# The first mixer's matrix products as three rounded products, with half of the modulation in later mixers

## What is computed

```python
proj = x @ w_in
da_q, da_k, da_v, r_q, r_k, r_v, r_g, m_q, gate_logits = split(proj)
y_da = diff_attention(da_q, da_k, da_v, ...)          # 8 heads, two softmaxes each
y_ret = silu(r_g) * retention(r_q, r_k, r_v, ...)     # 4 heads, a norm each
m_k, m_v = split(mem @ w_mem_kv)
y_mem = memory_attention(m_q, m_k, m_v)               # 4 heads
gates = sigmoid(gate_logits + b_gate)
merged = sum(gates[n] * (y[n] @ w_branch[n]) for n in range(3))
x = layer_norm(alpha * x + merged @ w_o)
```

## Time and profile before

| | |
|---|---|
| median of 3 runs | 2375.59 us (2375.39 to 2376.65) |
| the profiled execution | 2377.7 us, its span 2375.9 us |
| PE busy | 2269.4 us, 96% of the span |
| DVE busy | 1608.5 us, 68% |
| ACT busy | 1297.5 us, 55% |
| DMA | 638.14 MB, mean 269 GB/s |

### The profile page before, as it was taken

How to read it: one execution, slowest core, us unless ns; L and a number is a source line. 1 busy time by engine, 2 the same in 40 slices (tenths; PEclk the granted TensorE clock), 3 DMA queues, 4 the chain that set the end, 5 groups by cost and what they waited for, 6 DMA issues and landing times.

```text
span 2375.9 us, 25462 instructions
## 1 busy us (share of the span) xinstructions
PE 2269.4 (96%) x10290; PEld 1857.8 (78%) x10290; DVE 1608.5 (68%) x1897; ACT 1297.5 (55%) x1562; POOL 0.4 (0%) x6
## 2 busy tenths in 40 slices
PE   8999999998999979799989899999999999999997
PEld 7668877887888866578848788888888888888886
DVE  0266233546889863345423698989898998989895
ACT  1245113105677743334320587877777787878784
POOL 0000000000000000000000000000000000000000
PEclk9999999997999999999999799999999999999999
DMA  8465455745998862045440498999999898989892
GB/s 345 185 255 213 178 212 233 274 195 223 359 356 327 325 266 107 1 177 213 161 176 1 194 391 335 365 347 354 349 353 377 325 372 327 374 328 376 326 374 96
DMA packets 51217, 638.14 MB, mean 269 GB/s; under 512 B 8737, under 2 KB 10638, under 8 KB 12302
## 3 DMA queue, kind: packets, MB, share of 16 engines
q1 hardware_dynamic: 48526, 630.33, 69.1%
q10 hardware_dynamic: 2560, 6.03, 0.7%
HBM read 635.29 MB, written 1.05 MB: 268 GB/s over the span
## 4 chain that ended last, share of the span: by engine, by line
PE 91%; DVE 4%; ACT 2%; DMA 2%; issue 1%; SPq 0%; DVEq 0%; ACTq 0%
PE psum L1697 56%; PE psum L1487 19%; PE psum L1479 5%; PE psum L1707 2%; PE psum L1581 2%; PE psum L1720 2%; PE psum L1787 2%; DMA ring<-w_in 1%; DMA ring<-w_branch_in 1%; DVE stage_lo L1338 1%; PE psum L1592 0%; ACT arena L546 0%; DMA ring<-w_in_in 0%; DVE arena L559 0%; PE psum L1509 0%
## 5 line engine op out<-in xcount | busy, mean ns | idle before, releaser
L1338 DVE TENSOR_TENSOR stage_lo<-ring,stage_hi 128x1024 fp32r<-128x1024 f32 (+1 forms) x934 | 1109.6, 1218 | 107.4 <-ACT stage_hi L926 82.7
L926 ACT ACTIVATE stage_hi<-ring 128x1024 fp32r<-128x1024 f32 (+1 forms) x934 | 965.3, 1056 | 279.0 <-PE psum L1697 247.9
L1697 PE MATMUL psum<-stage_hi,x_hi 128*128 128x512 f32 (+1 forms) x1344 | 529.1, 394 | 14.2 <-DVE x_lo L1320 11.5
L1697 PE MATMUL psum<-stage_hi,x_lo 128*128 128x512 f32 (+1 forms) x1344 | 522.3, 389 | 0.0
L1697 PE MATMUL psum<-stage_lo,x_hi 128*128 128x512 f32 (+1 forms) x1344 | 521.1, 388 | 0.0
L1697 PEld LDWEIGHTS psum<-stage_hi,x_hi 128*128 128x128 f32 x1344 | 253.2, 188 | 64.1 <-issue 11.9
L1697 PEld LDWEIGHTS psum<-stage_hi,x_lo 128*128 128x128 f32 x1344 | 253.0, 188 | 53.0
L1697 PEld LDWEIGHTS psum<-stage_lo,x_hi 128*128 128x128 f32 x1344 | 253.5, 189 | 49.3
L1697 PE MATMUL psum<-stage_hi,h_hi 128*128 128x512 f32 x664 | 259.9, 391 | 4.8 <-DVE h_lo L1377 4.8
L1697 PE MATMUL psum<-stage_lo,h_hi 128*128 128x512 f32 x664 | 258.6, 389 | 0.0
L1487 PE MATMUL psum<-arena,ring 128*128 128x256 f32 x1024 | 227.0, 382 | 6.3 <-DVE arena L1285 4.3
(11 more groups left out here) (210 smaller groups left out, 1764.5 us busy)
## 6 DMA issues: line engine op xcount, KB each, us to landing
ring<-moe_w_gate_in SPq DMA_DIRECT2D x56, 2048.0 KB, 9.5
ring<-moe_w_up_in SPq DMA_DIRECT2D x56, 2048.0 KB, 9.6
ring<-moe_w_down_in SPq DMA_DIRECT2D x56, 2048.0 KB, 9.4
ring<-w_in SPq DMA_DIRECT2D x48, 2048.0 KB, 9.6
ring<-ada_w_in SPq DMA_DIRECT2D x15, 2048.0 KB, 7.9
ring<-w_in_in SPq DMA_DIRECT2D x14, 2048.0 KB, 10.8
mixer_tiles<-ada_w_in SPq DMA_DIRECT2D x9, 2048.0 KB, 7.9
mixer_tiles<-w_in_in SPq DMA_DIRECT2D x6, 2048.0 KB, 12.8
```

The costliest lines, as they stand in the source:

```text
L926: act.activation(chunk_view(stage_hi, f, side, p, c), chunk_source(f, side, p, c), ACT.Copy)\
L1338: dve.tensor_tensor(chunk_view(stage_lo, f, side, p, c), chunk_source(f, side, p, c), chunk_view(stage_hi, f, side, p, c).bitcast(F32), AL ...
L1697: ins = pe.matmul(dst, a, b, start=start, stop=stop)
```

## The change

Each of mixer 1's 64 products is done as three products of rounded operands, as in the feed-forward network. A new function, `with_stages`, puts a `stage` step in front of the gemm that comes before the one staged, and ahead of scores that stand there. In it ACT rounds the chunks (two of 1024 columns for a product, four for a value pair) to one of four buffers (`HIS`) in `mixer_tiles`, and DVE writes chunk minus rounded chunk over the weights in their slot. `split` steps do the same for the inputs x, y_da, mem, y_ret, y_mem and merged. PE waits for each chunk's low part, and ACT for the buffer of four chunks before. The value products (`TURNED`) are done two at a time.

The rounded inputs and the four buffers lie where slots 3 and 4 were, so mixer 1 has three slots. x and mem are laid out transposed by the host, which takes 16 transposes, their copies and the `turn` steps away; x is loaded a second time ahead of the last products. The small tables are loaded after the third panel. Of the 24 modulation steps 12 stay in mixer 1 (two among the keys, two behind the value pairs, four in the retention, four in the memory heads), six go to mixer 2 and six to mixer 3. Sums that stood at the top of DVE's program (lambda and gain) move behind the key products' vectors.

```diff
+TURNED = ("da_v", "r_v", "m_v")
+SPLIT_OF = {"branch0": "yda", "m_k": "mem", "m_v": "mem", "branch1": "yret", "branch2": "ymem", "w_o": "merged"}
+def with_stages(steps):
+    jobs = [n for n, q in enumerate(steps) if q[0] == "gemm" and not (q[1] in TURNED and q[2] % 2)]
+    at = {}
+    for before, n in zip([None] + jobs, jobs):
+        where = n if before is None else before
+        while where and steps[where - 1][0].endswith("_score"):
+            where -= 1
+        at.setdefault(where, []).append(("stage",) + steps[n][1:])
+    out = []
+    for n, q in enumerate(steps):
+        out += at.get(n, []) + [q]
+    return out
 def mixer1_steps():
-    s = [("turn_x", i, 0) for i in range(4)]
-    s += [("gemm", "da_q", i) for i in range(4)] + [("gemm", "da_k", i) for i in range(4)]
+    def splits(name, n=4):
+        return [("split", name, i) for i in range(n)]
+    def pairs(name, n):
+        return [[("gemm", name, i), ("gemm", name, i + 1)] for i in range(0, n, 2)]
+    def singles(*names):
+        return [[("gemm", n, i)] for n, k in names for i in range(k)]
+    s = splits("x")
+    s += [("gemm", "da_q", i) for i in range(4)]
     s += [("vec", 0, 0), ("vec", 1, 0)]
-    s += [("turn_mem", i, 0) for i in range(4)]
-    s += [("gemm", "da_v", i) for i in range(4)]
-    fill = [("gemm", n, i) for n, k in (("r_q", 2), ("r_k", 2), ("r_v", 4), ("r_g", 4), ("gate0", 4)) for i in range(k)]
+    for i in range(4):
+        s += [("gemm", "da_k", i)] + ([("ada", 0, i // 2)] if i % 2 else [])
+    for n, two in enumerate(pairs("da_v", 4)):
+        s += two + [("ada", 0, 2 + n)]
+    fill = singles(("r_q", 2), ("r_k", 2)) + [q for two in pairs("r_v", 4) for q in (two, [])]
+    fill += singles(("r_g", 4), ("gate0", 4))
     for h in range(DA_H):
-        s += [("da_score", h, 0), ("da_score", h, 1), fill.pop(0)]
+        s += [("da_score", h, 0), ("da_score", h, 1)] + fill.pop(0)
         if h:
-            s += [("da_norm", h - 1, 0)]
-        s += [fill.pop(0), ("da_turn", h, 0)] + ([("ada", 0, h)] if h < DA_H - 1 else []) + [("da_out", h, 0)]
-    s += [("ret_score", 0, 0), ("da_norm", DA_H - 1, 0)]
-    fill = [("gemm", n, i) for n, k in (("m_q", 4), ("m_k", 4), ("m_v", 4)) for i in range(k)]
-    s += [fill.pop(0), fill.pop(0)]
-    s += [("gemm", "branch0", i) for i in range(4)] + [("ada", 0, DA_H - 1)]
+            s += [("da_norm", h - 1, 0)] + ([("split", "yda", h // 2 - 1)] if h % 2 == 0 else [])
+        s += fill.pop(0) + [("da_turn", h, 0), ("da_out", h, 0)]
+    s += [("ret_score", 0, 0), ("da_norm", DA_H - 1, 0), ("split", "yda", 3)]
+    fill = singles(("m_q", 4), ("m_k", 4)) + pairs("m_v", 4)
+    s += fill.pop(0) + fill.pop(0)
+    s += [("gemm", "branch0", i) for i in range(4)] + splits("mem")
     for h in range(RET_H):
         if h:
-            s += [("ret_score", h, 0), fill.pop(0)]
-        s += [("ret_out", h, 0), fill.pop(0), ("ada", 0, DA_H + h), ("ret_mean", h, 0)] + fill[:1] + [("ret_var", h, 0)]
-        del fill[:1]
-    s += fill
-    fill = [("gemm", n, i) for n, k in (("gate1", 4), ("branch1", 4)) for i in range(k)]
+            s += [("ret_score", h, 0)] + fill.pop(0)
+        s += [("ret_out", h, 0)] + fill.pop(0) + [("ada", 0, 4 + h), ("ret_mean", h, 0)]
+        s += (fill.pop(0) if len(fill) > 2 * (RET_H - 1 - h) else []) + [("ret_var", h, 0)]
+    s += [q for one in fill for q in one] + splits("yret")
+    fill = singles(("gate1", 4), ("branch1", 4))
     for h in range(MEM_H):
-        s += [("mem_score", h, 0), fill.pop(0), ("mem_turn", h, 0), fill.pop(0), ("mem_out", h, 0), ("ada", 1, h)]
-    for n in ("gate2", "branch2"):
-        for i in range(4):
-            s += [("gemm", n, i)] + [("ada", 1, MEM_H + (4 if n == "branch2" else 0) + i)]
+        s += [("mem_score", h, 0)] + fill.pop(0) + [("mem_turn", h, 0)] + fill.pop(0) + [("mem_out", h, 0),
+                                                                                          ("ada", 0, 8 + h)]
+    s += splits("ymem")
+    s += [("gemm", "gate2", i) for i in range(4)]
+    for i in range(4):
+        s += [("gemm", "branch2", i), ("split", "merged", i)]
     s += [("gemm", "w_o", i) for i in range(4)]
     s += [("ln_sum", 0, 0), ("ln_sq", 0, 0), ("logits", 0, 0)]
     s += [("turn_tok", 0, i) for i in range(4)]
-    return s + [("rank", 0, 0)]
+    return with_stages(s + [("rank", 0, 0)])
...
 def mixer2_steps():
     s = [("ln_sum", 1, 0), ("ln_sq", 1, 0)]
-    s += [("gemm", "ev_q", i) for i in range(2)]
-    s += [("ev_k", 0, 0), ("ev_v", 0, 0), ("gqa_score", 0, 0), ("gqa_score", 1, 0)]
+    s += [q for i in range(2) for q in (("gemm", "ev_q", i), ("ada", 1, i))]
+    s += [("ev_k", 0, 0), ("ada", 1, 2), ("ev_v", 0, 0), ("gqa_score", 0, 0), ("gqa_score", 1, 0)]
     fill = [("gemm", "ev_p", 0), ("gemm", "ev_p", 1)] + [(n, i, 0) for n in ("pool", "pool_map") for i in range(2)]
     for h in range(GQA_H):
         s += fill[:1] + [("gqa_turn", h, 0)]
         del fill[:1]
         if h + 2 < GQA_H:
             s += [("gqa_score", h + 2, 0)]
-        s += [("gqa_out", h, 0)]
+        s += [("gqa_out", h, 0)] + ([("ada", 1, 3 + h // 2)] if h in (1, 3, 5) else [])
...
+    for n, name in enumerate(("od_v", "od_u")):
+        for i in range(4):
+            s += [("gemm", name, i)] + ([("ada", 1, 6 + 3 * n + i)] if i < 3 else [])
...
+M_X_HI, M_Y_HI, M_HI = 0, 2048, 4096
+HIS = 4
...
-            elif s == ("da_score", 0, 0) or s[0] == "ada" and s != ("ada", 1, 11):
-
-                m = 0 if s[0] == "da_score" else 12 * s[1] + s[2] + 1
-                key = ("ada", m // 12, m % 12)
-                src, free = w["ada_w_2"][m // 12, m % 12], (ada_summed, m + 1)
+            elif s[0] == "ada":
+                src, free = w["ada_w_2"][s[1], s[2]], (ada_summed, 12 * s[1] + s[2] + 1)
...
-        plan_loads(n, SLOTS)
+        plan_loads(n, SLOTS if n else FF_SLOTS)
...
+                if kind == "stage":
+                    for n, c in staged_chunks(s):
+                        at, fill = panel[("gemm", a, i - i % 2)]
+                        if c == 0:
+                            act.wait_ge(slot_full[at], 16 * fill)
+                        if n >= HIS:
+                            act.wait_ge(*chunk_use[n - HIS])
+                        act.activation(staged_hi(s, n), staged_source(s, c, ring), ACT.Copy).then_inc(w_hi_set, 1)
+                    continue
...
+                elif kind == "stage":
+                    for n, c in staged_chunks(s):
+                        dve.wait_ge(w_hi_set, n + 1)
+                        dve.tensor_tensor(staged_source(s, c, ring_split), staged_source(s, c, ring),
+                                          staged_hi(s, n).bitcast(F32), ALU.subtract).then_inc(w_lo_set, 1)
+                elif kind == "split":
+                    from_, hi, lo = (v[:, 2 * i:2 * i + 2, :] for v in split_tiles[a])
+                    dve.wait_ge(in_hi_set, split_at[(a, i)])
+                    dve.tensor_tensor(lo, from_, hi.bitcast(F32), ALU.subtract).then_inc(in_lo_set, 1)
...
+        def split_product(s):
+            _, a, i = s
+            _, x_hi, x_lo = split_tiles[split_name(a)]
+            if a in TURNED:
+                nxt = ("gemm", a, i + 1)
+                banks = [open_bank(s), open_bank(nxt)]
+                for n, c in staged_chunks(s):
+                    pe.wait_ge(w_lo_set, n + 1)
+                    hi, lo = staged_hi(s, n), staged_source(s, c, ring_split)
+                    for t in range(TB):
+                        tokens = slice(t * P, (t + 1) * P)
+                        for k in range(2):
+                            if i == 0 and t == 0:
+                                pe.wait_ge(in_lo_set, split_at[(split_name(a), c)])
+                            for m, (wt, xt) in enumerate(((hi, x_hi), (lo, x_hi), (hi, x_lo))):
+                                ins = pe.matmul(bank(banks[t]), xt[:, 2 * c + k, tokens], wt[:, k, :],
+                                                start=(c + k + m == 0), stop=(c == 3 and k == 1 and m == 2))
+                        if c == 3:
+                            ins.then_inc(job_done, 1)
+                    if c < 3:
+                        ins.then_inc(w_used, 1)
+                return
+            b = open_bank(s)
+            for m, (n, c) in enumerate(staged_chunks(s)):
+                pe.wait_ge(w_lo_set, n + 1)
+                hi, lo = staged_hi(s, n), staged_source(s, c, ring_split)
+                for k in range(KT):
+                    if i == 0 and m == 0 and k % 2 == 0:
+                        pe.wait_ge(in_lo_set, split_at[(split_name(a), k // 2)])
+                    for j, (wt, xt) in enumerate(((hi, x_hi), (hi, x_lo), (lo, x_hi))):
+                        ins = pe.matmul(bank(b, 2, T)[:, m, :], wt[:, k, :], xt[:, k, :], start=(k + j == 0),
+                                        stop=(k == KT - 1 and j == 2))
+                ins.then_inc(w_used if m == 0 else job_done, 1)
```

## The result

The changed kernel takes 2433.65 us (median of 4 runs, 2429.16 to 2435.82), the kernel before on the same chip 2375.49. The ratio is 1.024 (95% interval 1.0227 to 1.0253), 58 us. The forecast was 2407, within a range of 2362 to 2445: the sign and most of the mechanism held, and the forecast change, 31.5 us, was about half of the measured one. The profiled execution is the shortest of the four (2429.16 us, span 2427.2), so the traces differ by 51.3 us.

The account below looks back on a forecast made before the run. By sums PE still bounds, but products wait for in-order staging on ACT and DVE. Terms 8.8 + 23.0 - 6.7 + 11.7 - 3.2 - 14.1 + 3.0 + 8.6 = +31.1 give 2408.8, less 2.1: 2407 us; range 2362 to 2445.

Parts of the forecast that it names:

- What the products cost PE: Mixer 1: 52 products save 62 us and six value pairs 17.5, so PE work falls by 79.5 us.
- PE busy down by about 80 us: Sign expected on the profile page after: PE busy about 80 us lower, with more idle time than that added.
- The start and the first section: Mixer 1's start: first product at about 18.6 us, waits at da_v 0, da_v 2 and r_q; plus 8.8 us.
- Heads: Mixer 1, heads 1 to 7: chunks staged ahead of softmaxes, head 2 27.6 us, head 3 19.2; plus 23 us.
- Prelude, tail and mixer 2: Faster products: prelude minus 6.7 us, tail minus 14.1; modulations behind softmaxes in mixer 2: plus 8.6.
- Retention and memory: Mixer 1: retention plus 11.7 us, eleven products saving 14.2 against waits of 25.9; memory heads minus 3.2, eight products.
- rival B: Mixer 1: modulation panels in a three-slot chain, twelve steps not hidden, 59 us more: 2466 us; chance 0.10.
- Clock: Mixer 1: PE's clock lower after one or two waits as long as 4.32 us; plus 3 us.
- Rival A: Mixer 1: staging on ACT and DVE hides, heads stay PE-bound, about 2302 us; chance of this side 0.15.
- Rival C: Mixer 1's heads: a table load holds ACT another 1.28 us, fifteen switches cost 19 us: 2426 us; chance 0.07.
- Rival D: Mixer 1's products: still fp32, or no faster with chunk-strided weights, staying at 6.9 us each: 2469 us; chance 0.03.

## Why the forecast was right, and where it was short

- **What the products cost PE**: right. 425.5 us of PE work were forecast, 432.7 measured with the staging away. But the sign "PE busy down by about 80 us" did not come: it fell by 46, which is the clock's, below.
- **The start and the first section**: right as to the waits. 18.6 us for the first product, measured 18.89; waits of 4, 7.3 and one at r_q forecast, 5.41, 4.81 and 4.39 measured. Head 0's output ends at 127.90, and 124.2 was forecast.
- **Heads**: the mechanism was right to the place: a wait in one piece at head 2's turn, 9.70 us, and the block of four chunks behind it. From head 0's output to head 7's it was 148 us forecast, 154.7 measured (127.90 to 282.64). Nearly all of the miss is in heads 2 and 3, 30.5 and 22.6 where 27.6 and 19.2 were laid out, and these are the heads with the lowest granted clock, 0.73 and 0.80.
- **Prelude, tail and mixer 2**: -6.7, -14.1 and +8.6 forecast; -5.7, -12.5 and +9.8 measured. The experiments show mixer 2's part on its own twice.
- **Retention and memory**: +11.7 and -3.2 forecast, +17.2 and -0.2 measured. The stretch of the memory heads holds seven products and not the eight of the forecast, which is 1.2 us. For part of the rest see rival B.
- **Clock**: this is the term that was mis-sized. The step said "one or two waits as long in it: plus 3", though the same layout had four waits longer than the 4.32 us that it looked at (7.3, over 10, 7.8 and 8.5). PE waited over 3 us in 14 places of mixer 1, and its granted clock fell from 1.00 to 0.92: 13 pieces at the lower level, where the kernel before has one of 3.42 us. These 13 pieces together, and PE's work in them:

```profile
sum 85.33, PE 56.09; mean PE 4.31
```

  Work takes about twice as long there (the scores 1.98 us and not 1.14), so some 28 us are the clock's, an estimate from these numbers, where the forecast had 3. Without them PE's work is 428.7 us, and 425.5 had been worked out. The waits came to less than laid out, 89 us with the start against 99. So mixer 1 missed the forecast of +22.5 by 18.4: 25 for the clock, 3 for the rest of PE's work, less 10 for waits. The run without staging has 20.5 us at the lower level itself, which is why its work is only 24 us less and not 28. The run with filled waits shows 6 us won; how much more would come without any wait at half level is left open.
- **Rival A** (the staging hides) is what the rewritten list makes largely true, 2336 us where full hiding was put at 2302: it is a property of the order, not of the operations.
- **Rival B** came in small, in the retention and the memory heads. In the retention a panel lands 13.1 us after its issue, and the wait of 5.54 us at ret_var 1 stands behind its staging and the modulation after it. In the memory heads three times in a row the next panel is issued when a modulation has left its slot, lands 12.2, 9.8 and 7.9 us later, and the next modulation stands behind its staging. How much of the 58 us this is, no run shows. The chain that ended last, at that panel of the retention and then from one modulation of the memory heads to the next:

```profile
334.35 13.10 DMA ring<-w_mem_kv_in
...
439.75 1.13 DVE ring L1143
...
444.36 12.18 DMA ring<-w_branch_in
...
456.55 1.07 ACT mixer_split L834
...
457.65 2.36 DVE ring_split L1321 x2
460.01 1.14 DVE ring L1143
```

- **Rival C** falls: behind a root, which followed a load, a rounding starts at once. ACT in time, in the rewritten version:

```profile
130.11 1.28 ACT L953 ACT_TABLE_LOAD   x1
131.41 0.47 ACT L953 ACTIVATE mixer_tiles<-psum,arena 128x256 f32<-128x256 f32 x1
131.78 2.94 ACT L879 ACTIVATE mixer_split<-ring 128x1024 fp32r<-128x1024 f32 x3
```

No run shows a second 1.3 us behind a load; a rounding right behind a load occurs only at the start, where it waits for its input.
- **Rival D** falls by the changed kernel itself: with the real weights the last stretch of mixer 1 has 578 records in 69.38 us, 0.12 each.

## What to carry to other kernels

When PE's work is made cheaper at the price of work on other engines, sums of busy time say only what is possible; the result is set by where the new steps stand in each in-order program. Look for a step that waits for PE ahead of a step that PE waits for (here a buffer ring of four in front of a softmax): here it cost the full turn-around of the buffers, and moving it by one place was worth more than its own duration. Fill the gaps in which two engines hand work to and fro, and then count again.

## What the runs showed of the hardware beyond what was expected

PE's clock fell behind shorter waits than the one of 4.32 us that I had looked at: behind a wait of 3.03 us at head 1's output the scores took 1.98 us instead of 1.14. PE in time:

```profile
144.63 1.13 PE L1658 MATMUL psum<-mixer_tiles,arena 128*128 128x256 f32 x4 [3.03 <-ACT mixer_tiles L820]
145.69 1.98 PE L1645 MATMUL psum<-arena 64*128 64x256 f32 x8
```

The length of the wait alone does not tell. The kernel before waits 1.90 us ahead of ret_var 3, and so does the kernel with the modulations moved. What follows is slow in the first and not in the second:

```profile
370.75 3.54 PE L1553 MATMUL psum<-arena 128*128 128x256 f32 x8
...
370.70 1.89 PE L1556 MATMUL psum<-arena 128*128 128x256 f32 x8
```

Some 65 us of useless matmuls in the waits raised the granted clock of mixer 1 from 0.92 to 0.98, and the kernel was 12 us faster.
